# The last projection of a two-block network turned round: activations stationary, weights streamed, output stored by token

## What is computed

```python
mix = jnp.concatenate([att, cnv], axis=-1) @ w_out[l]          # [256, 1024] @ [1024, 1024]
x = x + gate[:, None, :] * rms_norm(mix, post_norm_g[l])       # the norm runs over the 1024 features
```

## Time and profile before

| | before |
|---|---|
| median of three runs | 822.70 us |
| the profiled execution's own time | 822.93 us |
| its span, first to last instruction | 821.0 us |
| TensorE (PE) busy | 804.1 us, 98% |
| VectorE (DVE) busy | 585.8 us, 71% |
| ScalarE (ACT) busy | 417.7 us, 51% |
| GpSimd (POOL) busy | 130.2 us, 16% |

### The profile page before, as it was taken

How to read it: one execution, slowest core, us unless ns; L and a number is a source line. 1 busy time by engine, 2 the same in 40 slices (tenths; PEclk the granted TensorE clock), 3 DMA queues, 4 the chain that set the end, 5 groups by cost and what they waited for, 6 DMA issues and landing times.

```text
span 821.0 us, 15756 instructions
## 1 busy us (share of the span) xinstructions
PE 804.1 (98%) x6452; PEld 780.0 (95%) x6452; DVE 585.8 (71%) x945; ACT 417.7 (51%) x717; POOL 130.2 (16%) x138
## 2 busy tenths in 40 slices
PE   9999999999999999999999999999999999999996
PEld 9999999999899898989999999999899998899995
DVE  6877776797687875798777768776667567567643
ACT  7444444544257664655444445536555454464541
POOL 3000000122210000020000003130245202036413
PEclk9999999999899999999999999999999999999999
DMA  8876776676245633449878875536444551835521
GB/s 330 314 256 227 243 249 230 233 259 205 89 134 188 209 104 103 154 154 334 304 277 270 289 246 180 192 92 210 160 144 142 168 179 48 261 129 156 154 77 52
DMA packets 45770, 158.91 MB, mean 194 GB/s; under 512 B 5075, under 2 KB 7635, under 8 KB 45699
## 3 DMA queue, kind: packets, MB, share of 16 engines
q1 hardware_dynamic: 45698, 157.92, 57.5%
HBM read 156.83 MB, written 1.06 MB: 192 GB/s over the span
## 4 chain that ended last, share of the span: by engine, by line
PE 80%; DVE 12%; ACT 5%; issue 2%; POOL 1%; DVEq 0%; ACTq 0%; POOLq 0%
PE ps L112 73%; PE ps L114 7%; DVE w L114 3%; DVE u L114 2%; ACT w L114 2%; DVE tmp L114 2%; DVE yg L114 1%; DVE cv L114 1%; ACT SW L114 1%; POOL rst L114 1%; ACT L114 1%; ACT ytm L114 1%; DVE Vs L114 0%; DVE hT L114 0%; DVE g L114 0%
## 5 line engine op out<-in xcount | busy, mean ns | idle before, releaser
L112 PE MATMUL ps<-u,w 128*128 128x256 f32 (+1 forms) x3887 | 502.0, 286 | 2.5 <-DVE w L114 1.2
L112 PEld LDWEIGHTS ps<-u,w 128*128 128x128 f32 x3887 | 483.7, 189 | 11.2 <-DVE w L114 3.2
L114 DVE TENSOR_TENSOR w<-raw,w 128x1024 fp32r<-128x1024 f32 x245 | 298.1, 1227 | 161.1 <-ACT w L114 160.1
L114 ACT CAST w<-raw 128x1024 fp32r<-128x1024 f32 x245 | 253.9, 1049 | 124.9 <-PE ps L114 116.5
L112 PE MATMUL ps<-h,w 128*128 128x272 f32 (+1 forms) x1000 | 130.4, 285 | 0.0
L112 PEld LDWEIGHTS ps<-h,w 128*128 128x128 f32 x1000 | 126.1, 188 | 0.1
L114 POOL TENSOR_TENSOR sqa<-sqa,sq 128x256 f32<-128x256 f32 (+1 forms) x22 | 22.7, 1031 | 357.5 <-ACT sq L114 357.0
L114 POOL TENSOR_SCALAR Sb<-Sb,st 128x256 f32<-128x256 f32 x32 | 45.0, 1422 | 89.1 <-DVE st L114 89.1
L114 DVE SCALAR_TENSOR_TENSOR acc<-adr,cact,acc 128x1024 f32<-128x1024 f32 x42 | 56.6, 1358 | 0.2 <-DMA adr<-wada 0.2
L114 PE MATMUL ps<-u,w 128*128 128x256 f32 (+1 forms) x169 | 48.1, 285 | 0.0
L112 PE MATMUL ps<-m,w 128*128 128x256 f32 x368 | 46.7, 281 | 0.0
(11 more groups left out here) (175 smaller groups left out, 698.1 us busy)
## 6 DMA issues: line engine op xcount, KB each, us to landing
raw<-wst SPq DMA_DIRECT2D x245, 512.0 KB, 4.6
adr<-wada SPq DMA_DIRECT2D x48, 512.0 KB, 4.2
Bt<-bias_rows SPq DMA_DIRECT2D x8, 192.0 KB
hT<-xT SPq DMA_DIRECT2D x4, 272.0 KB, 5.1
outT<-hT SPq DMA_DIRECT2D x2, 384.0 KB, 2.6
outT<-hT SPq DMA_DIRECT2D x1, 256.0 KB, 2.6
cs<-cst SPq DMA_DIRECT2D x1, 140.0 KB, 5.0
cs<-cst SPq DMA_DIRECT2D x1, 128.0 KB, 6.9
```

Source lines behind the costliest of these rows:

```text
L112: fn()
L114: fn().then_inc(m[0], m[1])
```

## The change

For layer 1 only, the last projection is by token. `token_outputs` keeps 128 tokens of `m1` or `m2` stationary and streams 512 columns of the weights; the products of 128 tokens by 1024 features fill two banks, and all four banks 0 to 3 are claimed before the first matmul. The chunks of this weight matrix are its rows, in the order of the tiles. For the first three chunks both halves of the tokens are done; for the last five first those of tokens 0 to 127, then eight transposes of `hT` into the banks 4 and 5, then those of tokens 128 to 255, then eight more transposes into the banks 6 and 7. `finish(t)` does the norm with tokens on the partitions and stores rows of 512 features. The gain as a row (`grow`) is made by eight transposes and two ScalarE copies in `rms_pair` of the boundary before, where they stand in place of a part of the filler matmuls. `rms_broadcast` and `add_back` go away.

```diff
@@ rms_pair
             if n == T:
                 bias_rows(0)
                 dense(1)
+            elif fill:
+                fill(0)
+                dense(1)
             else:
                 dense(4)
...
             if n == T:
                 bias_rows(1)
                 dense(3)
+            elif fill:
+                fill(1)
+                dense(3)
             else:
                 dense(6)
@@ before layer
+        def gain_rows(half):
+            b = take()
+            pe.wait(m_G[1], free[b])
+            for j in range(4):
+                k = 4 * half + j
+                m = pe(partial(nc.tensor.transpose, ps[:, b, 128 * j:128 * j + 128],
+                               GP2[:, 1, k:k + 1].broadcast_to([P, P]), ident))
+            last["g"] = free[b] = act(partial(nc.scalar.copy, grow[:, 512 * half:512 * half + 512], ps[:, b, :]), m)
+
+        def token_outputs(m1, m2, mx1, mx, hm):
+            order = (0, 1, 2, 4, 5, 6, 3, 7)
+            bank = [[take(), take()] for _ in range(2)]
+            done = {}
+            def products(i, c, t):
+                kt = order[i]
+                pe.wait(mx1[kt], mx[kt])
+                x, y = m1[:, kt, 128 * t:128 * t + 128], m2[:, kt, 128 * t:128 * t + 128]
+                for hf in range(2):
+                    a, b = w1[:, c % NW, 512 * hf:512 * hf + 512], w2[:, c % NW, 512 * hf:512 * hf + 512]
+                    out = ps[:, bank[t][hf], :]
+                    pe.quiet(partial(nc.tensor.matmul, out, x, a, start=i == 0, stop=False))
+                    pe.quiet(partial(nc.tensor.matmul, out, x, b, start=False, stop=False))
+                    done[t, hf] = pe(partial(nc.tensor.matmul, out, y, a, start=False, stop=i == KT - 1))
+                return done[t, 1]
+            def rows_of_h(t):
+                for k in range(KT):
+                    b = 4 + 2 * t + k // 4
+                    if k % 4 == 0:
+                        pe.wait(free[b], m_cst)
+                    last["h", t] = pe(partial(nc.tensor.transpose, ps[:, b, 128 * (k % 4):128 * (k % 4) + 128],
+                                              hT[:, k, 16 + 128 * t:144 + 128 * t], ident), hm[k])
+            st4 = sums[:, 0:4]
+            def finish(t):
+                gy = [ygf[:, 1024 * t + 512 * hf:1024 * t + 512 * hf + 512] for hf in range(2)]
+                for hf in range(2):
+                    src = ps[:, bank[t][hf], :]
+                    q = act(partial(nc.scalar.activation, gy[hf], src, ACT.Square, scale=1.0 / 32,
+                                    accum_out=st4[:, 2 * t + hf:2 * t + hf + 1]), done[t, hf])
+                    g = dve(partial(nc.vector.tensor_tensor, gy[hf], src, grow[:, 512 * hf:512 * hf + 512], ALU.mult),
+                            q, last["g"])
+                m = dve(partial(nc.vector.scalar_tensor_tensor, sst[:, t:t + 1], st4[:, 2 * t:2 * t + 1], EPS,
+                                st4[:, 2 * t + 1:2 * t + 2], ALU.add, ALU.add), q, state.get("pow"))
+                m = state["pow"] = pool(partial(nc.gpsimd.tensor_tensor, rst[:, t:t + 1], sst[:, t:t + 1],
+                                                eps3[:, t:t + 1], ALU.pow), m, m_eps, state.get("bc"))
+                dve.wait(g, m)
+                for hf in range(2):
+                    m = dve(partial(nc.vector.scalar_tensor_tensor, gy[hf], gy[hf], rst[:, t:t + 1],
+                                    ps[:, 4 + 2 * t + hf, :], ALU.mult, ALU.add), last["h", t])
+                    n_ = 2 * t + hf + 1
+                    m = sp.dma(partial(nc.sync.dma_start, outT[128 * t:128 * t + 128, 512 * hf:512 * hf + 512], gy[hf]),
+                               (s_out, 16 * n_), m)
+                return m
+            pe.wait(*[free[b] for b2 in bank for b in b2])
+            early = KT - NW
+            for i in range(early):
+                c = chunk()
+                products(i, c, 0)
+                done_chunk(c, products(i, c, 1))
+            cc = []
+            for i in range(early, KT):
+                cc.append(chunk())
+                products(i, cc[-1], 0)
+            rows_of_h(0)
+            finish(0)
+            for i, c in enumerate(cc):
+                products(early + i, c, 1)
+            rows_of_h(1)
+            return finish(1)
@@ layer, last statements
-            row_of_tiles(KT, KT, m1, m2, S, evac_mix(lambda j: GP2[:, l, j:j + 1], ygm, l == 0),
-                         (mx1, mx, (0, 1, 2, 4, 5, 6, 3, 7)), l == 0)
+            if l == 1:
+                return None, token_outputs(m1, m2, mx1, mx, hm)
+            row_of_tiles(KT, KT, m1, m2, S, evac_mix(lambda j: GP2[:, l, j:j + 1], ygm),
+                         (mx1, mx, (0, 1, 2, 4, 5, 6, 3, 7)))
```

More of the change, by code:

```diff
@@ L485, in spread, with rms_pair @@
             return mm
[L487 to L502, removed]
+        def rms_pair(n, eps_of=None, fill=None):
             nt = len(sum_tiles(n))
@@ L582, in normalise, with add_and_normalise @@
             return None
-        def add_and_normalise(n, off, ygm, hm, gain, shift, extra=None, eps_of=None):
-            r1, r2 = rms_pair(n, eps_of)
+        def add_and_normalise(n, off, ygm, hm, gain, shift, extra=None, eps_of=None, fill=None):
+            r1, r2 = rms_pair(n, eps_of, fill)
             mul, res = {}, {}
@@ L862, in ffn @@
             return ygm
[L864 to L881, removed]
         def vg(i):
@@ L1146, in layer_gains @@
             return m_G
+        ygf = yg[:, :, :].rearrange("p k t -> p (k t)")
+        grow = sq[:, :, :].rearrange("p k t -> p (k t)")[:, 0:D]
+        last = {}
+        def gain_rows(half):
[6 more added lines that the diff above has]
+            last["g"] = free[b] = act(partial(nc.scalar.copy, grow[:, 512 * half:512 * half + 512], ps[:, b, :]), m)
@@ L1148, in layer @@
         def layer(l, ygm, hm):
             hm = add_and_normalise(S, 16, ygm, hm, lambda k: G2[:, l, k:k + 1],
-                                   lambda k: mod[:, 24 * l + k:24 * l + k + 1], m_G[l])
+                                   lambda k: mod[:, 24 * l + k:24 * l + k + 1], m_G[l],
+                                   None, gain_rows if l else None)
             if l == 0:
@@ L1332, in build @@
         ygm, hm = layer(0, ygm, hm)
[L1333 to L1337, removed]
+        _, m = layer(1, ygm, hm)
         sp.wait(m)
@@ L1402 @@
         parts.append(np.stack([q[0], q[2], q[1], q[3]], 1).reshape(16, P, CH))
-        parts.append(tiles(A(w_out_2)[l]))
+        if l == 0:
+            parts.append(tiles(A(w_out_2)[l]))
+        else:
+            parts.append(A(w_out_2)[l].reshape(KT, P, D)[[0, 1, 2, 4, 5, 6, 3, 7]])
     wst = np.ascontiguousarray(np.concatenate(parts, 0))
@@ L1422 @@
     aps = [nc.dram_tensor(k, list(v.shape), F32, kind="ExternalInput").ap() for k, v in arrays.items()]
-    out = nc.dram_tensor("outT", [P, KT, S], F32, kind="ExternalOutput").ap()
+    out = nc.dram_tensor("outT", [S, D], F32, kind="ExternalOutput").ap()
     build(nc, *aps, out)
     r = run_bass_kernel_spmd(nc, [arrays], core_ids=[0])
-    o = r.results[0]["outT"]
-    return np.ascontiguousarray(o.transpose(2, 1, 0).reshape(S, D)[None])
+    return np.ascontiguousarray(r.results[0]["outT"][None])
```

## The result

The changed kernel takes 820.33 us (median of 7 runs, 820.13 to 820.52) against 822.81 us in the runs beside it (median of 7, 822.55 to 823.09): 0.9969 of the time before, 95% interval 0.9960 to 0.9978. It is faster by 2.5 us, and the interval excludes no change. The forecast was 820.7 us in a range of 819.6 to 822.6. The profiled execution took 820.19 us with a span of 818.4.

A forecast was written before the change was run, and what follows sets the result against it. TensorE, busy 98% of the span, was taken as the bound, with a serial chain after its last product. Last product 1.18 us later, 3.19 less after it: 2.01 saved from 822.70, so 820.7 us, range 819.6 to 822.6.

The forecast's parts named there:

- first product after the last block's: Start of last projection: waiting for the last block's bank makes TensorE's first product start 1.08 us late, at 788.90.
- spacing of 95 intervals: Last projection: 96 products of 512 columns, 0.2317 us apart as in the values' projection, 22.01 us to the last start.
- eight transposes of h: TensorE, before the second half's products in the last projection: 0.72 us, upper bound 0.94.
- last product's end, later than before: End of TensorE's last projection: last product ends at 812.15, 1.18 us later than before the change.
- power with its hand-offs: GpSimd's power in the tail for tokens 128 to 255: 0.08 + 0.73 + 0.05 = 0.86 us.
- I keep 3.01 us: Last 256 KB store: 3.01 us from last element to span's end, as before; possible queueing -0.3 to +0.4.
- the first tokens' stores: Sign of being right: stores of tokens 0 to 127 issued near 809, under TensorE's second pass.
- the clock rival: Boundary before layer 1: TensorE's clock falls, net 2.2 us lost, 822.9 us; chance 15%.
- three boundaries with fillers of 4 and 6: Argument against a clock fall before layer 1: none of these three boundaries in the trace shows the clock below full.
- Rival 2: Tail after the last product is longer than summed, 1.1 us in all with store queueing, 821.8 us; chance 15%.
- Rival 3: Wait at the projection's start is hidden, fourth bank read sooner or another bank waited for, 819.5 us; chance 7%.
- Rival 4: Tokens 0 to 127 not finished under the second pass, 3.8 us more at the end, 824.5 us; chance 3%.

The follow-up runs named there:

- experiment 1: Changed kernel with each bank waited for just before the first product that writes it, instead of all four at once; 819.34 us (0.9957).
- experiment 2: Changed kernel without the pass ahead: all eight chunks do both token halves and the two finishes follow one another; 821.70 us (0.9986).
- experiment 3: Changed kernel with the sum of accumulators plus eps moved ahead of the second gain multiplication on VectorE; 819.68 us (0.9965).
- experiment 5: Two runs: changed kernel with results and stores in 1 KB pieces, 820.70 us; kernel before with four equal 256 KB stores, 822.21 us.
- experiment 7: Changed kernel with bank waits just before use and the earlier sum, 818.60 us; the same with more fillers at the boundaries, 818.46 us.
- experiment 4: Changed kernel with the first eight transposes of h moved ahead of the wait for the four banks; 820.08 us (0.9962).
- experiment 6: Changed kernel without the four fillers beside the gain's transposes before layer 1, 820.72 us; without the head's six as well, 821.39 us.
- both edits: Changed kernel with bank waits just before use and the sum ahead of the second gain multiplication together; 818.60 us (0.9945).

## Why the prediction was right

By its own steps, as the profile has them:

| step | predicted | measured |
|---|---|---|
| first product after the last block's | 1.20 | 1.30 |
| spacing of 95 intervals | 0.2317, 22.01 us | 0.2333, 22.17 us |
| eight transposes of h | 0.72 | 805.00 - 803.98 - 0.23 = 0.79 |
| last product's end, later than before | 1.18 | 1.56 |
| hand-off, square, accumulator, gain | 1.47 | 813.71 - 812.26 = 1.45 |
| plus eps, not overlapped | 0.09 | 813.78 - 813.71 = 0.07 |
| power with its hand-offs | 0.86 | 814.51 - 813.78 = 0.73 |
| two multiply-and-adds | 1.41 | 1.41 |
| last product to last element | 3.83 | 3.66 |
| last element to the end | 3.01 | 2.48 |
| saved at the end | 2.01 | 2.33 |

The mechanism was right, as experiments 1 to 3 show one by one. Three terms were mis-sized. TensorE's path was 0.38 us too short in the sum: 0.10 at the hand-off, 0.16 in the spacing, 0.07 in the transposes, and the rest in the two restarts, of which the sum had one (the range had room for it). The tail was 0.17 us too long, 0.13 of it the power with its hand-offs: it was priced with the row of two columns (0.72, written 0.73 in the sum), and one column takes 0.56. The store was 0.53 us too long. The step "I keep 3.01 us" took the old store for one like the new; it feared that the last store would queue behind the one before, and missed that the old one already did so, with 384 KB ahead of it. It also had the old stores 1.3 us apart, where the last was issued 0.74 us after its forerunner (experiment 5). The first two errors are of opposite sign, and the store's makes up the rest. That they offset each other, so that the forecast came within 0.4 us of the measured 820.33, is luck.

Two readings were off without a part in the sum. The page shows one slice of the clock below full, not two. And the first tokens' stores were issued from 807.42, not near 809; the prediction's own terms put the first near 807.6 (the first pass ends at 804.48, and the tail up to the end of the first multiply-and-add takes 3.16).

The prediction placed the clock rival at 15% and 822.9 us. The changed kernel's own profile shows no fall there; the clock fell over the same boundary code in experiment 7, but was back before the products began, and it cost 0.33 us, not 2.2. The price came from the boundary with 272 tokens, where 59 products took 2.0 us longer than at full rate. But products ran at half rate for only 2.9 us of that fall (220.65 to 223.6), worth some 1.5 us by an estimate (half of 2.9); the rest are waits between products, which the changed kernel's profile has too. Between profiles the longer fall there, 6.8 against 3.4 us, cost 0.3 us. At the boundary before layer 1 a fall of 6.8 us cost 0.9 and 1.6 us, with products at half rate for 2.8 and 4.2 us of it.

Of the arguments against the rival one was weak. That three boundaries with fillers of 4 and 6 kept the clock was true of one execution; the profile of experiment 4 has it at 0.91 from 340 to 360, with exactly those fillers, and so have that of experiment 6 with six fillers left and that of both edits. The Trainium skill (TensorE: Matmul & The Clock Gate, Part 4: PE-mode transpose) says that transposes do not count as activity for the clock. With transposes alone, experiment 6 had it at 0.70 from 679 to 683 and 0.56 from 683 to 688, and a median 1.1 us worse: that agrees, though it does not show that they count for nothing, as TensorE was idle for longer too.

Rival 2, the longer tail, is refuted by the rows. Rival 3, a hidden wait, is refuted by the gap of 1.02 us that VectorE ended, and experiment 1 shows what it would have been worth. Rival 4 is refuted by the stores issued from 807.42, and experiment 2 gives its price as 1.4 us, not 3.8: it had counted a whole second finish, while the first one begins before the last product ends, so that the tail grows by 2.17 us, and it had not taken off the 0.79 us of transposes that leave TensorE's path.

The square and the gain multiplication of one half stay in series here. The Trainium skill (PSUM — Partial Sum Buffer, Terms, on the bank) says that two engines may not use one bank and quadrant at once, reads against reads included; no run here tried it, and experiment 3 got the overlap from the other half's work instead.

## What to carry to other kernels

Where a kernel ends in a reduction over its last result, give the reduction the axis that needs no matmul and no spread, and finish the first half of the rows under the second half's products; here that cut 7.0 us after the last product to 3.7. When several PSUM banks are claimed at once, wait for each just before its first write, since the youngest is still being read. Make the last store no larger than it must be, with none larger just ahead of it. Price a fall of the clock by the real products that run during it, less the waits that they would have had anyway, and give fillers no more than the wait that they stand in.

## What was not expected of the hardware

- The landing time of a 256 KB store was 2.6 us with one of 384 KB issued 0.74 us ahead, 2.2 us with an equal one 0.75 us ahead in the same 1 KB pieces, and 2.1 us with pieces of 2 KB.
- GpSimd's power took 0.72 us on two columns and 0.56 us on one.
- The half-rate stretch at one and the same boundary with 272 tokens lasted 6.8 us in one execution (216.8 to 223.6) and 3.4 us in another (0.68 in the slice from 219, 0.61 in that from 222), and the stretch over it differed by 0.31 us only (35.02 and 34.71).
